# A hybrid decoder step: the branch gates of its scan stage as half-size block products

## What is computed

```python
xn = rmsnorm(x, norm_mix)
u = xn @ w_in
u_fox, u_rw, u_gate = jnp.split(u, (FOX_COLS, FOX_COLS + RW_COLS), axis=-1)
...
g = jax.nn.sigmoid(gl) @ g2
...
wkv_new, o = lax.scan(_wkv_step, wkv_prev.astype(f32), xs)
...
g_a, g_b = jnp.split(jax.nn.sigmoid(u_gate), 2, axis=-1)
mixed = (g_a * (o_a.reshape(B, T, W_A) @ p_a) + g_b * (o_b @ p_b)) @ w_o
x = x + mixed
x = x + hier_moe(rmsnorm(x, norm_ffn), w_grp, w_exp, we_gate, we_up, we_down)
```

## Time and profile before

| what | us |
|---|---|
| time, median of 3 runs | 1702.08 (1694.32 to 1703.6) |
| span of the profiled execution | 1650.8 |
| median less that span | 51.3 |
| PE busy in the span | 1533.3 (93%) |
| DVE / ACT / POOL busy | 648.2 / 364.8 / 363.9 |
| scan stage, from its first product on PE to the next stage's first | 682.3 to 1011.5 |

### The profile page before, as it was taken

One profiled execution on the slowest core, in us unless ns is written; L12 is line 12 of the kernel. 1 busy time (PEld: TensorE's weight loads), 2 busy tenths in 40 slices (PEclk: granted clock), 3 DMA queues, 4 the chain that ended last, 5 costly groups with the idle time before them and its releaser, 6 DMA issues. The chain is left out here.

```text
span 1650.8 us, 29328 instructions
## 1 busy us (share of the span) xinstructions
PE 1533.3 (93%) x12183; PEld 895.8 (54%) x12183; DVE 648.2 (39%) x1348; ACT 364.8 (22%) x711; POOL 363.9 (22%) x417
## 2 busy tenths in 40 slices
PE   7999998989999999999999999999999399999992
PEld 4664454554878888667667765444554233333320
DVE  4203144433156458434633332345566322222225
ACT  3002144444122332012211111121112111111122
POOL 3001056654200000143242210001311331111123
PEclk9999999999999999999999999999999599999996
DMA  6603299999432211342231114443401789999996
GB/s 231 231 34 115 84 326 336 374 340 349 124 113 79 77 64 41 93 126 78 59 94 45 58 39 174 145 171 105 190 26 46 262 274 420 399 400 409 398 324 241
DMA packets 104438, 309.25 MB, mean 187 GB/s; under 512 B 29272, under 2 KB 39704, under 8 KB 93776
## 3 DMA queue, kind: packets, MB, share of 16 engines
q1 hardware_dynamic: 76928, 232.80, 38.5%
q0 software_dynamic: 26080, 70.26, 13.2%
q10 hardware_dynamic: 1296, 4.29, 0.7%
HBM read 259.02 MB, written 56.14 MB: 191 GB/s over the span
## 5 line engine op out<-in xcount | busy, mean ns | idle before, releaser
L1178 PE MATMUL rw_pp<-rows,rw_w 128*128 128x264 f32 x960 | 217.7, 387 | 0.0
L1495 PE MATMUL gate_p<-rows,gate_w 128*128 128x352 f32 x672 | 206.4, 463 | 0.4 <-DMA gate_w<-in_w_in 0.4
L1178 PEld LDWEIGHTS rw_pp<-rows,rw_w 128*128 128x128 f32 x960 | 181.6, 190 | 33.4 <-issue 2.8
L1495 PEld LDWEIGHTS gate_p<-rows,gate_w 128*128 128x128 f32 x672 | 125.4, 190 | 72.2 <-ACT u_rw L1645 5.2
L2318 PE MATMUL x_p<-wgu,rows 128*32 128x512 f32 (+1 forms) x640 | 123.6, 607 | 2.7 <-DMA wgu<-in_we_gu 1.4
L2318 PE MATMUL x_p<-late,rows 128*32 128x512 f32 (+1 forms) x640 | 122.6, 599 | 0.0
L1460 POOL DMA_DIRECT2D t_ring<-t_blocks x128 | 69.3, 549 | 138.7 <-DVE tt L1714 136.0
L458 POOL DMA_INDIRECT rows<-in_cache_kT,page_index x41 | 42.0, 1025 | 190.8 <-PE fox_b L514 102.4
L2336 ACT ACTIVATE rows<-h_p,vec 128x128 f32<-128x128 f32 x96 | 27.3, 367 | 245.1 <-PE h_p L2313 245.1
L2345 DVE SCALAR_TENSOR_TENSOR obT<-x_p,moe_ent,late 128x1024 f32<-128x1024 f32 x24 | 30.8, 1284 | 116.7 <-PE x_p L2330 116.7
L2295 POOL DMA_INDIRECT y<-obT,moe_ent x24 | 24.4, 1016 | 231.2 <-DVE obT L2345 203.3
(11 more groups left out here) (478 smaller groups left out, 2530.0 us busy)
## 6 DMA issues: line engine op xcount, KB each, us to landing
wgu<-in_we_gu SPq DMA_DIRECT2D x16, 2048.0 KB, 12.8
late<-in_we_gu SPq DMA_DIRECT2D x16, 2048.0 KB
wd<-in_we_down SPq DMA_DIRECT2D x16, 1024.0 KB, 19.3
late<-in_we_down SPq DMA_DIRECT2D x16, 1024.0 KB, 11.2
rows<-in_cache_kT SPq DMA_DIRECT2D x41, 256.0 KB, 7.5
gate_rows<-u_rw SPq DMA_DIRECT2D x54, 176.0 KB, 1.9
y<-const SPq DMA_DIRECT2D x9, 1024.0 KB, 6.3
rows<-in_cache_v SPq DMA_DIRECT2D x34, 256.0 KB, 7.2
```

What stands on the lines that cost most here:

```text
L1178: mm = pe.matmul(pp[u % 2][:, c, 0:QN], w[:, n % 2, k, :] if n else e.w_first[:, k, :], e.xnT[:, k, at:at + QN], start=(i == 0), stop=(i = ...
L1495: mm = pe.matmul(out[:, 0:GATE_N], gw[:, j % 2, k, :], e.xnT[:, k, at], start=(k == 0), stop=(k == KD - 1))
```

## The change

In the scan stage a pair of gate blocks (256 output columns) is made at once for half of the tokens. The weights of a pair fall into four quarters `a11`, `a12`, `a21`, `a22` (a block of columns by half of the 1024 inputs), the tokens' inputs into four quarters `b11` and so on (half of the inputs by 264 tokens). The four results of 264 tokens are made from seven products of quarters and of sums of quarters, in place of eight. There are 7 pairs by 2 token groups, which the diff calls 14 pairs, and 7 products in each. A product p.i below is product i (0 to 6) of pair p (0 to 13); it is four 128x128 by 128x264 products in one bank. The order of the work is:

- PE makes the 16 gain products (264 tokens each) first, then the 98 products. `FILLS` counts products: 43 before `across(0)` (16 gains, then 0.0 to 3.5), 2 after it, 4 in each of the rounds 1 to 15 and 5 in every third, and 1 and 3 in the last.
- POOL makes the weight sums of a pair by four subtractions or additions of 128x512 elements: `first_sums(p+1)`, two of them, at product p.5; `next_sum(p+1)` at p.6; `last_sum(p)` at p.1. Product p.1 needs the sum of `first_sums`, p.3 that of `next_sum`, p.4 that of `last_sum`.
- DVE makes the four token sums of the first group ahead of its solve; POOL makes those of the second group (128x4x264 each) during pair 6.
- ACT copies product p.0 and the gains to four slots. DVE adds the other six products from their PSUM bank to the slots (`adds`). Before a bank is written again, PE waits for the copy or the add of the product two before. In DVE's program the first adds are spread over `solve(0)` by `FIRST_ADDS`; in the rounds they stand between `centre`, `normalise` and the solve steps.
- Each slot is stored when its last add is done. Weights come as quarters of 256 KB, into four of six places; the attention's output `oaT` gives up its memory, so it is stored to HBM (2.2 MB) in `stage_rwkv_front` and loaded back when pair 6 is done.

```diff
-GATE_N, GATE_RING = NT // 3, 3
+GATE_N = NT // 4
...
+GAINS, PAIRS, NPROD = 4 * HP, KD - 1, 7
+PRODUCTS = GAINS + 2 * PAIRS * NPROD
+ADDED = list(accumulate(int(n >= GAINS and (n - GAINS) % NPROD > 0) for n in range(PRODUCTS)))
+KEPT = [n + 1 - x for n, x in enumerate(ADDED)]
+FIRST_FILLS, LAST_FILLS = (43, 2), (1, 3)
+FILLS = [sum(FIRST_FILLS)] + [4 + (c % 3 == 0) for c in range(1, NCH)] + [sum(LAST_FILLS)]
+FILLED = list(accumulate(FILLS))
+BLOCKS_AT, RING_AT = 30, 36
+FIRST_ADDS = [max(0, GAINS + int((x * 0.76 - 3.0) / 1.78)) if x > 5 else 0 for x in range(1, SUB)] + [30]
...
             for n in range(3, len(ORDER) + GATES // 2):
+                if n == 6:
+                    sp.wait_ge(divided, HP)
+                    sp.dma_start(e.oa_d, e.oaT).then_inc(stored, 16)
...
+            def first_sums(pair):
+                for name in ("a11", "a21"):
+                    pool.wait_ge(w_loaded[PLACES[pair][name]], 16 * loads_of(pair, PLACES[pair][name]))
+                pool.tensor_tensor(at("a21"), at("a11"), at("a21"), ALU.subtract).then_inc(w_summed, 1)
+                pool.wait_ge(w_loaded[PLACES[pair]["a22"]], 16 * loads_of(pair, PLACES[pair]["a22"]))
+                if pair:
+                    pool.wait_ge(q["unit_made"], made_by(pair - 1, 5))
+                pool.wait_ge(w_summed, 4 * pair + 1)
+                pool.tensor_tensor(at("s2"), at("a22"), at("a21"), ALU.subtract).then_inc(w_summed, 1)
...
             load_blocks(0)
+            sums_upto(GAINS)
             pool.memset(ring[:], 0.0).then_inc(ring_zero, 1)
...
+            sums_upto(BLOCKS_AT)
             store_blocks(0)
-            for c in range(NCH):
+            sums_upto(RING_AT)
+            load_ring(0)
+            load_ring(1)
+            sums_upto(FILLED[0])
+            for c in range(RING_T, NCH):
                 if c == RING_T:
                     load_blocks(1)
                 if c == HALF_CH - 1:
                     store_blocks(1)
                 load_ring(c)
+                sums_upto(FILLED[c - 1])
...
+                    if n >= 2:
+                        emptied(pe, n - 2)
...
+                        if i in (1, 3, 4):
+                            pe.wait_ge(w_summed, 4 * pair + {1: 2, 3: 3, 4: 4}[i])
...
+                        for k in range(half_k):
+                            mm = pe.matmul(bank, weights_at(pair, name)[:, k], moving[g][:, k],
+                                           start=(k == 0), stop=(k == half_k - 1))
...
+            first, later = solve(0), solve(1)
+            for n in range(SUB - 1):
+                next(first)
+                adds_upto(FIRST_ADDS[n])
+            adds_upto(FIRST_ADDS[-1])
+            next(first)
...
                     new_state(m)
+                solves = SOLVE_STEPS.get(c, 0)
+                begun = FILLED[c - 1] if c else 0
+                if B:
+                    adds_upto(begun + 1)
                     normalise(m)
-                for _ in range(SOLVE_STEPS.get(c, 0)):
+                for x in range(2, FILLS[c]):
+                    for _ in range((solves + 2) // 3 if x > 2 else 0):
+                        if solves:
+                            next(later)
+                            solves -= 1
+                    adds_upto(begun + x)
+                for _ in range(solves):
                     next(later)
                 if A:
                     update(c, b)
                 if B:
                     add_gained(m)
+                adds_upto(FILLED[c])
```

More of the change, by code:

```diff
@@ L1121, in _ @@
             sp.dma_start(a["shift_out"], last[:]).then_inc(stored, 16)
-            sp.wait_ge(stored, 32)
+            sp.wait_ge(stored, 48)
             sp.wait_ge(y2_filled, 16 * NTT)
@@ L1403, in after, with emptied @@
                 eng.wait_ge(s, v)
+        def emptied(eng, n):
+            if n >= GAINS and (n - GAINS) % NPROD:
+                eng.wait_ge(q["unit_added"], ADDED[n])
+            else:
+                eng.wait_ge(q["unit_kept"], KEPT[n])
         @block.sync
         def _(sp):
-            for j in range(2, 4):
-                sp.dma_start(gw[:, j % 2], a["w_in"][22 + j]).then_inc(w_loaded[j % 2], 16)
-            sp.dma_start(g2w, a["g2"]).then_inc(g2_loaded, 16)
-            last_gain = max(n for n, (kind, _) in enumerate(UNITS) if kind == "gain")
@@ L1462, in _, with sums_upto @@
+            steps = sums()
+            summed = 0
+            def sums_upto(count):
+                nonlocal summed
+                while summed < count:
+                    summed = next(steps, PRODUCTS)
             load_blocks(0)
+            sums_upto(GAINS)
             pool.memset(ring[:], 0.0).then_inc(ring_zero, 1)
@@ L1502, in fill @@
+            steps = products()
             def fill(count):
@@ L1640, in keep_units @@
                 nonlocal kept
-                while kept < len(UNITS) and UNIT_STEPS[kept] <= done:
-                    n = kept
-                    act.wait_ge(q["unit_made"], n + 1)
-                    after(act, gate_stored[n % GATE_RING], 16 * (n // GATE_RING))
-                    act.copy(gate[:, n % GATE_RING], gp[n % 2][:, 0:GATE_N]).then_inc(q["unit_kept"], 1)
-                    kept += 1
+                for n in range(kept, done):
+                    pair, i = divmod(n - GAINS, NPROD)
+                    if n < GAINS or i == 0:
+                        x = n % 4 if n < GAINS else 0
+                        act.wait_ge(q["unit_made"], n + 1)
+                        after(act, gate_stored[x], 16 * (n // 4 if n < GAINS else 4 + pair))
+                        act.copy(gate[:, x], gp[n % 2][:, 0:GATE_N]).then_inc(q["unit_kept"], 1)
+                kept = max(kept, done)
             for c in range(NCH + 1):
@@ L1669, in _ @@
                 if A:
-                    keep_units(sum(FIRST_FILLS) + c * FILL)
-            for n in range(kept, len(UNITS)):
-                act.wait_ge(q["unit_made"], n + 1)
-                after(act, gate_stored[n % GATE_RING], 16 * (n // GATE_RING))
-                act.copy(gate[:, n % GATE_RING], gp[n % 2][:, 0:GATE_N]).then_inc(q["unit_kept"], 1)
+                    keep_units(FILLED[c])
+            keep_units(PRODUCTS)
         @block.vector
@@ L1749, in add_gained, with adds, adds_upto @@
                 ins.then_inc(q["o_stored"], 1)
-            for _ in solve(0):
-                pass
-            later = solve(1)
+            def adds():
+                for n in range(PRODUCTS):
+                    pair, i = divmod(n - GAINS, NPROD)
+                    if n >= GAINS and i:
+                        bank = gp[n % 2][:, 0:GATE_N]
+                        dve.wait_ge(q["unit_made"], n + 1)
+                        if i == 1:
+                            dve.wait_ge(q["unit_kept"], KEPT[n])
+                        else:
+                            dve.wait_ge(q["unit_added"], ADDED[n - 1])
+                        fresh = {1: 2, 3: 3, 4: 1}.get(i)
+                        if fresh:
+                            dve.wait_ge(gate_stored[fresh], 16 * (4 + pair))
+                        if i == 5:
+                            dve.tensor_tensor(gate[:, 2:4], gate[:, 2:4], bank.unsqueeze(1).to_broadcast([P, 2, GATE_N]),
+                                              ALU.add).then_inc(q["unit_added"], 1)
+                        else:
+                            to, of = {1: (2, 0), 2: (0, 0), 3: (3, 2), 4: (1, 3), 6: (2, 2)}[i]
+                            dve.tensor_tensor(gate[:, to], gate[:, of], bank, ALU.add).then_inc(q["unit_added"], 1)
+                    yield n + 1
+            steps = adds()
+            added = 0
+            def adds_upto(count):
+                nonlocal added
+                while added < count:
+                    added = next(steps, PRODUCTS)
+            first, later = solve(0), solve(1)
[4 more added lines that the diff above has]
+            next(first)
             for c in range(NCH + 1):
```

186 lines of the change are left out of this document (132 added, 54 removed).

## The result

The changed kernel takes **1750.2 us** (median of 4 runs, 1745.6 to 1759.7) against 1701.5 of the kernel before (4 runs, 1694.3 to 1703.6): 1.0315 times as long, 95% interval 1.0268 to 1.0361. The forecast had the sign, and was 26 us too low; the range ended at 1740.

A forecast was written before the change was run, and what follows sets the result against it. PE was taken to bound the kernel, with two partners less than a few microseconds behind. The terms -28.7 + 26 + 17 + 6 + 1.5 = +21.8 gave 1724 us against the median of 1702.1, range 1693 to 1740.

The forecast's parts named there:

- part 3: Solve steps in rounds 2 to 5: later `update` and turns of DVE with POOL's sums, +17, between 7.6 and 26.
- part 2: First filling, up to across(0): late gains, solve and POOL queue leave PE idle 10.4 and 5.8 us; +26 in all.
- Part 1: PE's filling work in the scan: fewer, smaller products at 1.81 us each, a gain of 28.7 us.
- part 5: Tail: in the last round product 13.5 waits for an add, and the last store follows an add; +1.5, 0 to 3.
- The forecast's 7.6: Rounds 2 to 5: lateness of `update` from adds and solve steps if POOL holds nothing up, 7.6 us.
- the first rival: Full turns: every POOL sum costs DVE its length; part 3 is 26, total 1733 us, chance 0.18.
- Part 4: Round 6: `last_sum` of pair 7 stands behind `store_blocks(1)` and `load_ring(7)`, so PE waits; +6, or +9 with part 3 low.
- the terms at nothing: Store of `oaT` in the front stage and its load in round 5: hidden, no cost; at most 12 us once.
- The second and third rivals: Second: no turns for short instructions, 1711 us, chance 0.18. Third: POOL back in time at 2.4, 1692 us, chance 0.17.

The follow-up runs named there:

- a_order: Changed kernel with first-filling adds 5 us later, next_sum(3) between two ring loads and last_sum(7) ahead of store_blocks(1): 1749.7 us, scan 376.9.
- a_tinysums: Changed kernel with GpSimd's weight sums of pairs 1 to 13 cut to one column in 128: 1729.7 us, scan 357.9.
- b_idle: Kernel before, with PE waiting for a chain of five tiny DMAs in rounds 8, 10, 12 and 14: 1720.0 us against 1695.6.

## Why the prediction was wrong in size

The forecast had the direction and the places of the waits, and its scan came out 29.2 us too short. The term that was sized worst is the turns of part 3, then the first filling of part 2.

**Part 1, less filling work: right.** In round 4, with no wait just ahead of them, five products run from 868.34 to 877.47, so 1.83 us each where 1.81 was taken:

```profile
868.34 5.61 PE L1633 MATMUL gate_p<-rows,gate_w 128*128 128x264 f32 x24
873.78 3.76 PE L1633 MATMUL gate_p<-rows 128*128 128x264 f32 x16
877.47 0.62 PE L1646 MATMUL scan_tok<-t_ring,ys 64*64 64x64 f32 x14
```

The rounds from across(7) on won 11.3 us in all against 18.3 by the forecast's terms, part 5 included. Of the time there, 1.5 us are the longer start of the mix stage (a gap of 3.96 us against 2.47) and 3.0 are short waits on adds, 1.05 of them in the last round; the rest I have not taken apart.

**Part 2, the first filling: right in its places, 8.5 us too small.** Against the forecast, step by step:

- The step that failed first is the gains: a store of 1.9 us was taken from the earlier trace rows's median. At this moment the loads of the blocks and of the weights keep the DMA engines busy, and ScalarE waited 6.36 us for the first slot. Product 0.0 started 19.9 us behind the stage's start, where 12.6 was forecast, and 1.6, which the stores follow, ended some 7 us later than forecast.
- So add 0.1, which is placed among the solve steps by a table of expected times, held VectorE for 5.67 us where 0.5 was forecast. `a_order` took that wait away, and at most 2.2 us at product 2.3 are its worth.
- The turns came to 4.4 us in the solve where 5.9 was taken (five instructions of 1.01 to 1.40 us). Right in kind; the 5.9 itself doesn't follow from the forecast's five sums at 1.1, which are 5.5.
- `store_blocks(0)` started 54.0 us behind the start (47.3 forecast), the next landing was quicker (the second copy came 8.9 us behind it, not 11.6), and the waits were 7.5 and 4.8 for the forecast's 10.4 and 5.8. So 2.3 started 3.9 us later than forecast. PE's slow products behind each wait, 6.7 instead of 3.7 us, were not in the forecast, and the stretch from 2.3 to across(0) is 4.6 us longer than forecast; filling those waits gave 1.7 us here.

**Part 3, rounds 2 to 5: the term that was mis-sized.** Forecast +17 between 7.6 and 26; measured 29.1 us in rounds 3 to 6 against rounds with nobody late, and 26.8 against the same rounds of before (68.2 us) less the filling that the change saves in them (8.5). The step that failed is "as adds and reductions have at most one SBUF input, and part of the sums will meet those". With it the forecast left 9.4 us for the turns (17 less 7.6). From across(2) to across(6) the sums take 24.1 us, and VectorE's instructions with two SBUF inputs take 16.3 us more than undisturbed: 10.5 in the solve steps, and 5.8 in two multiplies, one in `new_state` and one in `normalise`, which stand ahead of the steps in the same chain and were taken at their undisturbed length. The forecast's 7.6 and these 16.3 make 23.9; the other 3 to 5 us are not taken apart, and PE's slower products behind the waits are among them. VectorE's groups of the changed kernel from 826 to 930 us (count, busy us, mean ns of one):

```profile
L1864 DVE TENSOR_TENSOR state_t<-state_grown,chunk_decay 128x256 f32<-128x256 f32 x5 | 6.3, 1269 | 0.2
L1883 DVE TENSOR_TENSOR gn_sqr<-gn_cent_t,gn_stat 128x256 f32<-128x256 f32 x5 | 4.7, 938 | 0.2
L1835 DVE TENSOR_TENSOR t_blocks_sb<-t_blocks_sb,t_spare 128x238 f32<-128x238 f32 x2 | 2.9, 1456 | 0.1
L1835 DVE TENSOR_TENSOR t_blocks_sb<-t_blocks_sb,t_spare 128x130 f32<-128x130 f32 x2 | 2.7, 1343 | 0.1
L1913 DVE TENSOR_TENSOR u_rw<-u_rw,gate_p 128x264 f32<-128x264 f32 x16 | 6.8, 422 | 3.5 <-PE gate_p L1633 3.4
```

The multiplies take 1.27 and 0.94 us where each takes 0.42 alone, the two solve groups 1.46 and 1.34 where theirs take 0.41 and 0.29, while the adds keep their 0.42. So for this part the first rival, full turns, was the one that came true, and its 26 was about right; its total, 1733, was too low all the same, by the other parts. Making the weight sums small (11.1 us up to across(7)) or the solve (10.4 net) each gives a part, and with both, and the token sums small too, rounds 3 to 6 have no lateness left.

**Part 4, the loop's round 6: right in kind, 3.7 us too small.** The wait is 7.8 us and ended by `last_sum`, as forecast. The whole round came to 9.7 us more than before less its saved filling, where 6 was forecast; the products behind the wait are slow here too. Together the scan missed the forecast by 29.2 us: 8.5 in part 2, 9.8 in part 3, 3.7 in part 4, and 7.0 behind across(7), with 0.2 left.

**Part 5 and the terms at nothing: no miss found.** In the last round PE waited 1.05 us for the add, where 1.4 was forecast; whether the 1.5 us ahead of the mix stage are the last store's isn't shown. The front stage is as long with the store of `oaT` as without it. The load back is issued at 926.6, just ahead of `store_blocks(1)`. The first four DMAs of these stores then take 7.3 us to land (median) where they took 4.8 before, but GpSimd's wait between the halves is not longer (8.46 us against 10.08). No run leaves this load out.

The second and third rivals needed GpSimd and VectorE not to hold each other up, or GpSimd back in time at 2.4. `a_tinysums` is the nearest to the first of these in the changed order, and even that is 28.7 us above the scan of before.

The cause that is shown: turns of VectorE with GpSimd's sums, the solve steps beside them, and the order of stores, landings, ring loads and sums on in-order queues. Not shown: what the gains' lateness costs and what ends it (no run removed it), what PE's lower clock costs in rounds 3 to 6, and the timed rest in `b_idle`.

## What to carry to other kernels

An engine at 99% busy hides how close its partners are: before taking a twelfth of its work away at the price of work on two others, write down for each round the chain that must be done when it asks, with every two-operand instruction at the length that it has beside the neighbour's. A wait that an experiment removes for no gain is not thereby cheap; look at what ended the next one, which may be a wait that the move itself made (3.3 us for the order and 3.5 for the buffer alone, 20.3 with both and three further moves). And compare stages, not spans: one execution was 41 us off in a stage that nobody had touched.

## What was not expected of the hardware

- A VectorE instruction of 128x4 with two SBUF operands took 2.35 us beside a GpSimd sum of 128x1056, 0.16 without; an add with one operand in PSUM kept 0.41.
- PE's granted clock in the first filling was 0.84 with waits of 4.8 to 7.5 us, and products behind them took 6.7 instead of 3.7 us per sixteen, while waits of 1.6 to 2.7 us left the small products behind them at full speed (0.62 us) and one of 3.95 did not (1.01). Raising the clock there to 0.93 by useless products brought across(0) only 1.7 us forward, since PE was not what the filling waited for.
- A store of 16 bytes a row gave its slot back as late as one of 132 KB (waits of 5.70 and 6.36 us), while the DMA engines were busy: all of that time with the whole stores, and for the first 4 us of it with the small ones.
